# A hybrid decoder layer on eight cores: the norms as two sequences each, and attention's first query and key projections released by the first parked residual tile

## The chip, the cores and the metric

The kernel runs on the 8 cores of one Trainium2 chip. Each core computes one of the 8 batch elements with the same program and the same weights; the cores exchange nothing. The metric is the device time of the slowest core in microseconds (us), lower is better.

## The reference, cut to what is computed

```python
h = x + 0.5 * swiglu(rmsnorm(x, g1), w_gate_up1, w_down1)        # D=1024, D_FF=2816
u = rmsnorm(h, g_mix)
hg_q, hg_f, hg_i, hg_og, att_qkv, gate_A, gate_B = split(u @ w_in)
y_A = hgrn2(...)       # 4 heads, 128x128 state, chunks of 64, own norm and output gate
y_B = attention(...)   # 3 groups (window, dilation) = (128,1), (512,4), (2048,16), 8 heads of 64 each,
                       # causal, ALiBi; group outputs are joined by their softmax denominators
h = h + (sigmoid(gate_A) * (y_A @ w_A) + sigmoid(gate_B) * (y_B @ w_B)) @ w_out
h = h + 0.5 * swiglu(rmsnorm(h, g2), w_gate_up2, w_down2)
out = rmsnorm(h, g_final)
# rmsnorm(x, g) = x * rsqrt(mean(x*x) + 1e-6) * g;  x: (8, 2048, 1024) float32
```

## The kernel before, in words

**Layout.** A core keeps its 2048 tokens as 4 token tiles `tt` of 512, features on the partitions (8 chunks `c` of 128). The residual `hT` is one 64 KB-per-partition tile of float32 at offset H0, stored tile by tile; the normalized activations `xnT` are bf16 behind it. Weights are loaded in bf16 by POOL's DMA queue; the residual is parked in DRAM ("spill", L447) and the result stored (`store`, L453) by SP's queue.

**The planner.** Nothing is written out in engine order. Nineteen generators ("streams", list at L1141) yield small chunks of instructions or the name of an event to wait for. `schedule` (L182) takes, again and again, the chunk with the smallest key: its earliest start by a cost model (clock of its engine, readiness of its operands) plus the bias of its stream plus `P.extra`, a surcharge that a stream can put on its next chunk. Committed chunks go to the end of their engine's queue. Events order the commits only; what an instruction waits for on the chip comes from records (`Tok`, L31), one per buffer or part of one, that hold the last writer and the readers. `place` (L313) puts a buffer over older ones and takes over their records' readers and writers. Every engine's queue is in order. The planner takes 2 us plus bytes at 300 per ns for a DMA, 720 ns for a scalar-tensor-tensor (STT) of 512 columns on VectorE (DVE), 216 ns for a matmul of 512 columns.

**The norms.** `norm_stream` (L411) serves all four norms ("0" before the first feed-forward part, "1" before the mixer, "2" before the second feed-forward part, "3" the final one, in place). For each tile it squares the 8 chunks (`s_sq`, two buffers), adds each into bank 7 by a matmul with ones, takes Ln into `lnv` and Exp into bank 6, and multiplies the 8 chunks by gain and factor (8 STTs, surcharge 900 for norms 1 to 3 except on the last tile). Only then does it start the squares of the next tile. For norm 3 the last tile is done in two halves of 256 columns, as the last down projection is, yet both halves share one record per chunk.

**The first feed-forward part** (`ffn_stream`, L471) goes through gate-up and down weights in three groups. The last group's down projections (`down`, L509) go tile by tile: 8 pieces `m` of 8 matmuls, each followed by an STT into `hT`. Banks: 0 to 3 gate-up, 4, 5, 2, 3 the last downs, 7 norm sums, 6 norm factors.

**Around the change.** After that part the recurrence (`hg_proj` L569, `hg_vog` L636, `hg_state` L683) and attention run side by side. `hg_vog` projects values through bank 7 and waits for the event "norm1_done". `hg_state` needs them; its banks are 1 and 2. `at_load` (L801) waits for "ffn0_done" and "norm1_done", places attention's buffers over the residual (query and key tiles over residual tile 0, the others over tiles 1 to 3) and its weights over the down weights, sets the ones of the value tiles, and issues the bias and three weight DMAs (query, key, value) of each of 12 rounds `k`. `at_proj` (L837) projects them per round, 12 tiles of 8 matmuls through bank 3 (banks 2 and 3 once the recurrence is done), ScalarE (ACT) copies each out; `at_units` (L886) does scores and sums.

**The tail.** The second feed-forward part is the same code; its last down projections run over tiles 0, 1, 2 and the two halves of tile 3, and norm 3 and the stores follow.

Of the kernel before, what the change touches and what calls it, by code (L numbers as in the profile page):

```python
# [274 lines left out]
def build_program():  # L275
# [18 lines left out]
    with ExitStack() as st:  # L294
# [73 lines left out]
        hT_t = toks(8, 4)  # L368
        xn_t = toks(8, 4)
# [9 lines left out]
        hT = place("hT0", [128, 4, 8, 512], F32, H0, hT_t)  # L379
# [13 lines left out]
        def load_x():  # L393
            pre = ffn_pre(0)
            for tt in range(4):
                for q in range(4 if tt == 0 else 2):
                    n_ = 2 if tt == 0 else 4
                    DMA("pool", hT[:, tt, q * n_:(q + 1) * n_, :], xT_d[tt, :, q * n_ * 512:(q + 1) * n_ * 512], P.dsem(),
                        n_ * 262144, writes=[hT_t[c][tt] for c in range(q * n_, (q + 1) * n_)])
                    yield None  # L400
# [10 lines left out]
        def norm_stream(tag, gcol, inplace, after):  # L411
            for tt, lo, hi in ((0, 0, 512), (1, 0, 512), (2, 0, 512)) + (((3, 0, 256), (3, 256, 512)) if inplace else ((3, 0, 512),)):
                n_ = hi - lo
                for c in range(8):
# [5 lines left out]
                    if eng == "act":  # L420
                        ACT(sq[c % 2][:, 0:n_], h_[:, tt, c, lo:hi], AF.Square, [hT_t[c][tt]], [sq_t[c % 2]], n_)
                    else:
                        TT(eng, sq[c % 2][:, 0:n_], h_[:, tt, c, lo:hi], h_[:, tt, c, lo:hi], ALU.mult, [hT_t[c][tt]], [sq_t[c % 2]], costs[eng])
# [6 lines left out]
                yield None  # L430
                for c in range(8):
                    o_, ot = (h_[:, tt, c, lo:hi], hT_t[c][tt]) if inplace else (xnT[:, c, tsl(tt)], xn_t[c][tt])
                    STT(o_, h_[:, tt, c, lo:hi], vecs[:, gcol + c:gcol + c + 1], banks[6][:, 0:n_], ALU.mult, ALU.mult,
                        [hT_t[c][tt], bt[6], vecs_t], [ot], 55.0 + n_ * 1.3)
                    P.extra = 900.0 if tag != "0" and tt < 3 else 0.0
# [5 lines left out]
                P.events.add("xn%s_%d" % (tag, tt))  # L441
                if not inplace and after is not None:
                    after(tt)
                    yield None
            P.events.add("norm%s_done" % tag)

        def spill(tt):  # L447
            DMA("sp", hsp_d[tt], box["hT"][:, tt, :, :].rearrange("p c t -> p (c t)"), P.dsem(), 2097152,
                reads=[hT_t[c][tt] for c in range(8)], writes=[hsp_t[tt]])
# [3 lines left out]
        def store(tt, q, lo, hi):  # L453
            DMA("sp", outT_d[tt, :, q * 2048:(q + 1) * 2048].rearrange("p (c t) -> p c t", c=4)[:, :, lo:hi],
                box["hT"][:, tt, q * 4:(q + 1) * 4, lo:hi],
                out_ds[tt * 2 + q + (2 if lo else 0)], 2048 * (hi - lo), reads=[hT_t[c][tt] for c in range(q * 4, (q + 1) * 4)])
# [14 lines left out]
        def ffn_stream(which, xtag, htag):  # L471
# [37 lines left out]
            def down(grp, m, tt, dbs, lo=0, hi=512):  # L509
# [3 lines left out]
                for jj in range(n):  # L513
# [5 lines left out]
                    [bt[db], hT_t[m][tt]], [hT_t[m][tt]], 30.0 + (hi - lo) * 1.29)  # L519
# [281 lines left out]
        def at_load():  # L801
            yield "ffn0_done"
            yield "norm1_done"
# [6 lines left out]
            tmp_t, pT_t, acc_t = toks(2), toks(2, 4), toks(2, 4)  # L810
            at["qR"] = [place("qR%d" % i, [128, S], BF16, H0 + i * 4096, qR_t[i]) for i in range(2)]
            at["kR"] = [place("kR%d" % i, [128, S], BF16, H0 + 8192 + i * 4096, kR_t[i]) for i in range(2)]
            at["va"] = [place("vaug%d" % i, [128, 16, 2, 128], BF16, H0 + 16384 + i * 8192, va_t[i], vone_t[i]) for i in range(2)]
# [4 lines left out]
            at.update(qR_t=qR_t, kR_t=kR_t, vT_t=vT_t, va_t=va_t, vone_t=vone_t, tmp_t=tmp_t, pT_t=pT_t, acc_t=acc_t)  # L818
# [4 lines left out]
            for k in range(12):  # L823
# [6 lines left out]
                for s_ in range(3):  # L830
                    if k >= 1:
                        yield "part_%d_%d" % (k - 1, s_)
# [407 lines left out]
```

How the kernel before makes its waits and increments, by code:

```python
        def run(e, h):  # L234
            waited = {}
            for i, o in enumerate(prog.ops[e]):
                for ev in o["waits"]:
                    if ev[0] == "E":
                        sem, val, key = prog.esem[ev[1]], prog._resolve(ev), ("E", ev[1])
                    else:
                        sem, val, key = ev[1].h, ev[2], ("D", id(ev[1]))
                    if waited.get(key, 0) >= val:
                        continue
                    waited[key] = val
                    h.wait_ge(sem, val)
                if o["fn"] is None:
                    continue
                inst = o["fn"](h)
                if o["kind"] == "d":
                    inst.then_inc(o["ds"].h, 16)
                elif i in prog.needed[e]:
                    inst.then_inc(prog.esem[e], 1)
```

## Time and profile before

| | us |
|---|---|
| median of 3 runs | 1766.26 |
| all runs | 1763.83, 1766.26, 1945.64 |
| the profiled execution | 1766.38 |
| its span, slowest core (core 4), first to last instruction | 1764.8 |
| spans of the eight cores | 1757.6 to 1764.8 |
| TensorE busy (95% of the span) | 1674.9 |
| VectorE (DVE), ScalarE (ACT), GpSimd (POOL) busy | 769.3, 618.6, 167.4 |
| mean granted TensorE clock, core 4 | 0.980 |

The profile is one execution, seen on its slowest core. In its rows L336 is the helper through which all matmuls go, L342 ScalarE's activations, L348 the STTs, L360 the DMAs; the names `out<-in` tell them apart. "PEld" is TensorE's weight load, beside its matmuls. "x8" is a count; brackets or the part behind the bar give the idle time of the engine just before and what ended it. Matmuls are pipelined, so a matmul's own length (0.38 us) is more than its share of time.

### The profile page before, as it was taken

The page shows a single profiled execution, that of the slowest core. Times are in us where ns is not written, and L with a number is a line of the kernel's source. Part 1 is how long each engine was busy: PE and PEld are TensorE (multiplying, and loading weights), DVE is VectorE, ACT ScalarE, POOL GpSimd, SP SyncE. Part 2 cuts the span into 40 slices and gives each one's busy share as a digit, 9 for nine tenths or more (in the row PEclk, how much of TensorE's full clock was granted, in tenths as well). Part 3 has the DMA queues.
Part 4 walks back from the last instruction along what each step waited for, and adds up shares of the span by engine and source line. Part 5 has one row for each costly group of instructions (what it writes and reads, how often), then busy time and mean ns, then how long its engine had stood idle before and what let it go on. Part 6 is the DMA issues. An engine that isn't in the chain of part 4 may idle for free.

```text
span 1764.8 us, 25674 instructions; the slowest of 8 cores (1757.6 to 1764.8 us)
## 1 busy us (share of the span) xinstructions
PE 1674.9 (95%) x8556; PEld 765.3 (43%) x8556; DVE 769.3 (44%) x1248; ACT 618.6 (35%) x1044; POOL 167.4 (9%) x315
## 2 busy tenths in 40 slices
PE   6999999999989898899999999799999999999996
PEld 2444444444434444444444444344444444444443
DVE  4424223312465565764555445554632322331245
ACT  4310110011335666666575575522421011001123
POOL 2200101100003333310000000000010010010000
PEclk9999999999989899999999999799999999999997
DMA  8420427320240000022221222652042032132013
GB/s 230 78 36 13 66 37 120 60 36 13 96 126 13 7 12 14 1 55 45 34 37 22 52 40 38 161 122 36 1 66 48 13 59 44 24 57 40 12 48 144
DMA packets 29600, 95.17 MB, mean 54 GB/s; under 512 B 3232, under 2 KB 5408, under 8 KB 26912
## 3 DMA queue, kind: packets, MB, share of 16 engines
q0 software_dynamic: 23472, 65.19, 21.6%
q1 hardware_dynamic: 6000, 28.34, 4.5%
q8 instruction: 73, 1.20, 0.3%
q14 instruction: 55, 0.45, 0.1%
HBM read 133.52 MB, written 16.78 MB: 85 GB/s over the span
## 4 chain that ended last, share of the span: by engine, by line
PE 88%; ACT 6%; issue 3%; DVE 2%; POOL 0%; DMA 0%; DVEq 0%; ACTq 0%; POOLq 0%
PE bank L336 87%; ACT s_fin L342 1%; ACT s_sq L342 1%; PE bank L339 1%; ACT s_T L342 1%; ACT s_lnv L342 1%; DVE s_hT L348 1%; DVE s_tmp L345 1%; ACT s_vT L342 0%; ACT L342 0%; DMA s_hT<-xT 0%; DVE s_T L620 0%; ACT s_vaug L342 0%; ACT s_kR L342 0%; DVE s_S L348 0%
## 5 line engine op out<-in xcount | busy, mean ns | idle before, releaser
L336 PE MATMUL bank<-s_xnT,s_wgu 128*128 128x512 bf16 x2816 | 618.7, 381 | 2.7 <-DVE s_xnT L348 2.4
L336 PEld LDWEIGHTS bank<-s_xnT,s_wgu 128*128 128x128 bf16 x2816 | 276.6, 98 | 340.2 <-issue 12.2
L342 ACT ACTIVATE s_sg<-bank 128x512 f32<-128x512 f32 x176 | 105.0, 597 | 659.0 <-PE bank L336 657.3
L345 DVE TENSOR_TENSOR s_actT<-s_sg,bank 128x512 bf16<-128x512 f32 x176 | 120.9, 688 | 463.4 <-PE bank L336 463.4
L336 PE MATMUL bank<-s_actT,s_wd 128*128 128x512 bf16 (+1 forms) x1472 | 309.3, 370 | 0.0
L336 PE MATMUL bank<-s_xnT,s_watt 128*128 128x512 bf16 x1152 | 285.3, 384 | 12.9 <-ACT s_kR L342 5.8
L348 DVE SCALAR_TENSOR_TENSOR s_hT<-bank,s_hT 128x512 f32<-128x512 f32 (+1 forms) x232 | 156.2, 673 | 195.0 <-PE bank L336 194.7
L336 PEld LDWEIGHTS bank<-s_actT,s_wd 128*128 128x128 bf16 x1472 | 143.7, 98 | 157.9 <-issue 0.6
L336 PEld LDWEIGHTS bank<-s_xnT,s_watt 128*128 128x128 bf16 x1152 | 105.0, 98 | 135.2 <-issue 30.9
L336 PE MATMUL bank<-s_xnT,s_wm 128*128 128x512 bf16 x512 | 128.0, 385 | 6.0 <-ACT s_sA L342 6.0
L345 DVE TENSOR_TENSOR s_tmp<-bank,s_bias 128x512 f32<-128x512 f32 (+1 forms) x200 | 104.4, 553 | 53.4 <-PE bank L336 40.1
L342 ACT ACTIVATE s_sq<-s_hT 128x512 bf16<-128x512 f32 (+1 forms) x121 | 69.0, 595 | 142.7 <-PE bank L336 88.9
L342 ACT ACTIVATE s_pT<-s_tmp 128x512 bf16<-128x512 f32 (+1 forms) x160 | 93.7, 601 | 53.2 <-DVE s_tmp L345 51.0
L336 PE MATMUL bank<-s_xnT,s_whg 128*128 128x512 bf16 x384 | 93.1, 379 | 0.5 <-ACT s_v L342 0.5
L336 PE MATMUL bank<-s_sq,s_ones_bf 128*128 128x512 bf16 (+1 forms) x136 | 51.3, 408 | 31.0 <-ACT s_sq L342 18.1
L336 PEld LDWEIGHTS bank<-s_xnT,s_wm 128*128 128x128 bf16 x512 | 48.9, 99 | 63.5 <-issue 12.3
L348 DVE SCALAR_TENSOR_TENSOR s_xnT<-s_hT,s_vecs,bank 128x512 bf16<-128x512 f32 x96 | 66.4, 741 | 13.6 <-ACT bank L342 13.6
L360 POOL DMA_DIRECT2D s_wgu<-wgu x44 | 23.3, 531 | 495.6 <-PE bank L336 495.4
L342 ACT ACTIVATE s_sA<-bank 128x512 f32<-128x512 f32 x64 | 38.1, 595 | 75.8 <-PE bank L336 73.7
L345 DVE TENSOR_TENSOR s_acc<-s_acc,bank 128x512 f32<-128x512 f32 x64 | 54.8, 892 | 22.3 <-PE bank L336 22.0
L351 POOL TENSOR_SCALAR s_Sb<-s_S,s_dcs 128x128 bf16<-128x128 f32 x112 | 48.1, 431 | 159.5 <-DVE s_S L348 107.0
L336 PE MATMUL bank<-s_mT,s_wo 128*128 128x512 bf16 x256 | 59.8, 379 | 0.0
(87 smaller groups left out, 1164.5 us busy)
## 6 DMA issues: line engine op xcount, KB each, us to landing
s_wgu<-wgu POOLq DMA_DIRECT2D x44, 512.0 KB, 5.2
s_wd<-wd POOLq DMA_DIRECT2D x44, 256.0 KB, 9.6
s_watt<-watt POOLq DMA_DIRECT2D x36, 256.0 KB, 4.0
hsp<-s_hT SPq DMA_DIRECT2D x4, 2048.0 KB, 6.3
s_hT<-hsp SPq DMA_DIRECT2D x4, 2048.0 KB, 25.5
s_hT<-xT POOLq DMA_DIRECT2D x6, 1024.0 KB, 26.4
outT<-s_hT SPq DMA_DIRECT2D x6, 1024.0 KB, 4.3
s_whg<-whg POOLq DMA_DIRECT2D x8, 512.0 KB, 21.0
```

What stands on the lines that cost most here:

```text
L336: P.op("pe", lambda h: h.matmul(out, lhsT=lhsT, rhs=rhs, start=start, stop=stop, skip_group_check=skip), reads, writes, mm_ns(n))
L339: P.op("pe", lambda h: h.transpose(out, in_, ident_), reads, writes, mm_ns(128))
L342: P.op("act", lambda h: h.activation(out=out, in_=in_, func=func, **kw), reads, writes, act_ns(n), TABLES.get(func))
L345: P.op(eng, lambda h: h.tensor_tensor(out=out, in0=in0, in1=in1, op=op), reads, writes, ns)
L348: P.op("dve", lambda h: h.scalar_tensor_tensor(out=out, in0=in0, scalar=scalar, in1=in1, op0=op0, op1=op1), reads, writes, ns)
L351: P.op(eng, lambda h: h.tensor_scalar(out=out, in0=in0, scalar1=s1, scalar2=s2, op0=op0, op1=op1), reads, writes, ns)
L360: return lambda h: h.dma_start(out=out, in_=in_)
```

## The change

1. `norm_stream` becomes two streams for each norm. `norm_sum` does squares, sums, Ln and Exp; `norm_apply` does the STTs and what follows them. The Exp writes banks in turn (6 and 5; 6 and 1; 6 alone; 6 and 0), and from the point where a bank is used again the sum sequence waits for the event that its earlier factors are applied. The sum streams of norms 1 and 3 get bias -700 (the other streams of the norms -300). The surcharge of 900 now also stands on the first half of norm 3's last tile.
2. The last 256 columns of the residual's tile 3 get records of their own (`hTb_t`), and every access goes through `ht(c, tt, lo, hi)`; the placements of the residual list their records per tile.
3. `at_load` waits for "norm1_done" later. The three weight DMAs of round 0 come at "ffn0_done"; the query and key tiles are placed once tile 0 is parked (event "sp_0"); the other buffers, the ones and the bias wait for "norm1_done" as before. `at_proj` starts at "at_qk", waits before each tile for that tile's normalized activations, and for "at_ready" before the first value projection.

```diff
+        hTb_t = toks(8)
+        def ht(c, tt, lo=0, hi=512):
+            if tt < 3:
+                return [hT_t[c][tt]]
+            return ([hT_t[c][tt]] if lo == 0 else []) + ([hTb_t[c]] if hi == 512 else [])
...
-        hT = place("hT0", [128, 4, 8, 512], F32, H0, hT_t)
+        hT = place("hT0", [128, 4, 8, 512], F32, H0, hT_t, hTb_t)
+        placed[-1:] = [(H0 + tt * 16384, H0 + (tt + 1) * 16384, [t for c in range(8) for t in ht(c, tt)]) for tt in range(4)]
...
-        def norm_stream(tag, gcol, inplace, after):
-            for tt, lo, hi in ((0, 0, 512), (1, 0, 512), (2, 0, 512)) + (((3, 0, 256), (3, 256, 512)) if inplace else ((3, 0, 512),)):
+        def norm_sum(tag, inplace, rbanks):
+            for i, (tt, lo, hi) in enumerate(norm_parts(inplace)):
                 n_ = hi - lo
+                rb = rbanks[i % len(rbanks)]
                 for c in range(8):
...
                     MM(banks[7][:, 0:n_], ones_bf[:], sq[c % 2][:, 0:n_], c == 0, c == 7, [sq_t[c % 2], ones_t], [bt[7]], n_)
                     yield None
+                if i >= len(rbanks):
+                    yield "na%s_%d" % (tag, i - len(rbanks))
                 ACT(lnv[:, 0:n_], banks[7][:, 0:n_], AF.Ln, [bt[7]], [lnv_t], n_, scale=1.0 / D, bias=EPS)
                 yield None
-                ACT(banks[6][:, 0:n_], lnv[:, 0:n_], AF.Exp, [lnv_t], [bt[6]], n_, scale=-0.5)
-                yield None
+                ACT(banks[rb][:, 0:n_], lnv[:, 0:n_], AF.Exp, [lnv_t], [bt[rb]], n_, scale=-0.5)
+                yield None
+                P.events.add("ns%s_%d" % (tag, i))
+
+        def norm_apply(tag, gcol, inplace, rbanks, after):
+            for i, (tt, lo, hi) in enumerate(norm_parts(inplace)):
...
+                yield "ns%s_%d" % (tag, i)
+                h_ = box["hT"]
                 for c in range(8):
...
-                    P.extra = 900.0 if tag != "0" and tt < 3 else 0.0
+                    P.extra = 900.0 if tag != "0" and hi < 512 or tt < 3 and tag != "0" else 0.0
...
+                P.events.add("na%s_%d" % (tag, i))
                 if not inplace and after is not None:
                     after(tt)
                     yield None
+                    P.events.add("sp_%d" % tt)
...
         def at_load():
             yield "ffn0_done"
-            yield "norm1_done"
...
+            for s_ in range(3):
+                first(0, s_)
+                yield None
+                P.events.add("watt_0_%d" % s_)
+            yield "sp_0"
             at["qR"] = [place("qR%d" % i, [128, S], BF16, H0 + i * 4096, qR_t[i]) for i in range(2)]
             at["kR"] = [place("kR%d" % i, [128, S], BF16, H0 + 8192 + i * 4096, kR_t[i]) for i in range(2)]
+            at.update(qR_t=qR_t, kR_t=kR_t)
+            P.events.add("at_qk")
+            yield "norm1_done"
...
         def at_proj():
-            yield "at_ready"
+            yield "at_qk"
...
                 for s_ in range(3):
                     yield "watt_%d_%d" % (k, s_)
...
+                    if s_ == 2 and k == 0:
+                        yield "at_ready"
...
                     for tt in range(4):
+                        yield "xn1_%d" % tt
                         B = nextb()
...
-            Stream("n0", norm_stream("0", 0, False, None), -300.0),
+            Stream("n0", norm_sum("0", False, (6, 5)), -300.0),
+            Stream("a0", norm_apply("0", 0, False, (6, 5), None), -300.0),
...
-            Stream("n1", norm_stream("1", 8, False, spill), -300.0),
+            Stream("n1", norm_sum("1", False, (6, 1)), -700.0),
+            Stream("a1", norm_apply("1", 8, False, (6, 1), spill), -300.0),
...
-            Stream("n3", norm_stream("3", 24, True, store), -300.0),
+            Stream("n3", norm_sum("3", True, (6, 0)), -700.0),
+            Stream("a3", norm_apply("3", 24, True, (6, 0), store), -300.0),
```

## Rows read from the trace of the kernel before

**Rows 1.** The page's chain that ended last, shares of the span by engine

```profile
PE 88%; ACT 6%; issue 3%; DVE 2%; POOL 0%; DMA 0%; DVEq 0%; ACTq 0%; POOLq 0%
```

**Rows 2.** Busy time by stretch; the first line names the columns

```profile
core 4: us, PE busy (x) PEld busy (x) DVE busy (x) ACT busy (x) POOL busy (x), PEclk, DMA share, GB/s
440.00:506.00 66.00, 65.53 (x302) 29.13 (x301) 37.33 (x55) 23.61 (x39) 2.55 (x2) 1.00 0.23 96
506.00:524.00 18.00, 11.54 (x31) 2.98 (x28) 11.40 (x17) 9.25 (x16) 1.65 (x3) 0.72 0.76 190
540.00:800.00 260.00, 234.85 (x1501) 111.99 (x1499) 165.55 (x329) 167.35 (x293) 74.00 (x143) 0.97 0.11 18
1225.00:1300.00 75.00, 74.07 (x338) 32.43 (x337) 38.57 (x57) 29.39 (x45) 2.35 (x5) 1.00 0.04 9
...
1740.00:1765.00 25.00, 8.14 (x23) 2.24 (x22) 16.12 (x31) 12.34 (x28) 0.00 (x0) 0.62 0.67 252
```

**Rows 3.** Start of the kernel, the same columns, 50 to 54 us

```profile
50.00:54.00 4.00, 2.02 (x6) 0.67 (x7) 3.47 (x6) 2.35 (x4) 3.12 (x5) 0.88 0.00 0
```

**Rows 4.** Instructions in order of time, end of the first feed-forward and after

```profile
506.59 0.69 DVE L348 SCALAR_TENSOR_TENSOR s_hT<-bank,s_hT 128x512 f32<-128x512 f32 x1 [1.47 <-PE bank L336]
...
507.10 1.65 POOL L360 DMA_DIRECT2D s_watt<-watt  x3 [17.92 <-PE bank L336]
507.37 0.32 SPq L360 DMA_DIRECT2D hsp<-s_hT  x1
...
510.02 5.36 DVE L348 SCALAR_TENSOR_TENSOR s_xnT<-s_hT,s_vecs,bank 128x512 bf16<-128x512 f32 x8 [2.74 <-ACT bank L342]
...
516.91 3.57 PE L336 MATMUL bank<-s_whg,s_xnT 128*128 128x512 bf16 x8 [0.84 <-ACT s_lnv L342]
```

**Rows 5.** Chain of waits, one round of down projection, sum and square

```profile
446.51 0.23 issue
446.74 0.70 DVE s_hT L348
...
447.64 0.64 ACT s_sq L342
...
448.41 0.59 PE bank L336 x2
```

**Rows 6.** Page, DMA issues: operation, count, KB each, median us to landing

```profile
s_watt<-watt POOLq DMA_DIRECT2D x36, 256.0 KB, 4.0
hsp<-s_hT SPq DMA_DIRECT2D x4, 2048.0 KB, 6.3
```

**Rows 7.** The attention weights' tile: issue to landing, window 500 to 530

```profile
DMA to landing us min/median/max: 11.3/13.2/14.8
```

**Rows 8.** DMA answer, window 507 to 525, issues and time to landing

```profile
hsp<-s_hT SPq DMA_DIRECT2D x1, 2048.0 KB, 11.2
```

**Rows 9.** Two single microseconds of the same stretch, columns as in Rows 2

```profile
511.00:512.00 1.00, 0.70 (x2) 0.10 (x1) 1.00 (x2) 0.72 (x2) 0.00 (x0) 0.50 1.19 236
521.00:522.00 1.00, 0.68 (x4) 0.35 (x5) 1.00 (x3) 0.18 (x1) 0.00 (x0) 1.00 0.95 240
```

**Rows 10.** Instructions in order of time, the tail

```profile
1739.96 0.42 DVE L348 SCALAR_TENSOR_TENSOR s_hT<-bank,s_hT 128x256 f32<-128x256 f32 x1 [0.45 <-PE bank L336]
...
1740.30 4.03 DVE L348 SCALAR_TENSOR_TENSOR s_hT<-s_hT,s_vecs,bank 128x512 f32<-128x512 f32 x6
...
1746.09 5.35 DVE L348 SCALAR_TENSOR_TENSOR s_hT<-s_hT,s_vecs,bank 128x512 f32<-128x512 f32 x8 [1.77 <-ACT bank L342]
...
1755.69 0.81 ACT L342 ACTIVATE s_sq<-s_hT 128x256 bf16<-128x256 f32 x2 [0.22 <-PE bank L336]
...
1758.15 3.22 DVE L348 SCALAR_TENSOR_TENSOR s_hT<-s_hT,s_vecs,bank 128x256 f32<-128x256 f32 x8 [2.90 <-ACT bank L342]
```

**Rows 11.** Groups by shape, window 1726 to 1766

```profile
L348 DVE SCALAR_TENSOR_TENSOR s_hT<-bank,s_hT 128x256 f32<-128x256 f32 x16 | 6.8, 424 | 7.0 <-PE bank L336 7.0
...
L342 ACT ACTIVATE s_sq<-s_hT 128x256 bf16<-128x256 f32 x16 | 6.1, 411 | 2.2 <-PE bank L336 1.6 <-DVE s_hT L348 0.7
```

More of the change, by code:

```diff
@@ L398, in load_x @@
                     DMA("pool", hT[:, tt, q * n_:(q + 1) * n_, :], xT_d[tt, :, q * n_ * 512:(q + 1) * n_ * 512], P.dsem(),
-                        n_ * 262144, writes=[hT_t[c][tt] for c in range(q * n_, (q + 1) * n_)])
+                        n_ * 262144, writes=[ht(c, tt) for c in range(q * n_, (q + 1) * n_)])
                     yield None
@@ L409, in load_x, with norm_parts @@
                     P.events.add("h0_%d_%d_0" % (c, tt))
-        def norm_stream(tag, gcol, inplace, after):
-            for tt, lo, hi in ((0, 0, 512), (1, 0, 512), (2, 0, 512)) + (((3, 0, 256), (3, 256, 512)) if inplace else ((3, 0, 512),)):
+        def norm_parts(inplace):
+            last = ((3, 0, 256), (3, 256, 512)) if inplace else ((3, 0, 512),)
+            return ((0, 0, 512), (1, 0, 512), (2, 0, 512)) + last
+        def norm_sum(tag, inplace, rbanks):
+            for i, (tt, lo, hi) in enumerate(norm_parts(inplace)):
                 n_ = hi - lo
+                rb = rbanks[i % len(rbanks)]
                 for c in range(8):
@@ L448, in spill @@
             DMA("sp", hsp_d[tt], box["hT"][:, tt, :, :].rearrange("p c t -> p (c t)"), P.dsem(), 2097152,
-                reads=[hT_t[c][tt] for c in range(8)], writes=[hsp_t[tt]])
+                reads=[ht(c, tt) for c in range(8)], writes=[hsp_t[tt]])
         out_ds = [P.dsem() for _ in range(10)]
@@ L455, in store @@
                 box["hT"][:, tt, q * 4:(q + 1) * 4, lo:hi],
-                out_ds[tt * 2 + q + (2 if lo else 0)], 2048 * (hi - lo), reads=[hT_t[c][tt] for c in range(q * 4, (q + 1) * 4)])
+                out_ds[tt * 2 + q + (2 if lo else 0)], 2048 * (hi - lo), reads=[ht(c, tt, lo, hi) for c in range(q * 4, (q + 1) * 4)])
         ffn_box = {}
@@ L810, in at_load, with first @@
             tmp_t, pT_t, acc_t = toks(2), toks(2, 4), toks(2, 4)
+            def first(k, s_):
+                DMA("pool", at["w"][s_][:], watt_d[k // 3, 2 - k % 3, s_], dsw[s_], 524288, writes=[w_t[s_]])
+            for s_ in range(3):
[3 more added lines that the diff above has]
+            yield "sp_0"
             at["qR"] = [place("qR%d" % i, [128, S], BF16, H0 + i * 4096, qR_t[i]) for i in range(2)]
             at["kR"] = [place("kR%d" % i, [128, S], BF16, H0 + 8192 + i * 4096, kR_t[i]) for i in range(2)]
+            at.update(qR_t=qR_t, kR_t=kR_t)
+            P.events.add("at_qk")
+            yield "norm1_done"
             at["va"] = [place("vaug%d" % i, [128, 16, 2, 128], BF16, H0 + 16384 + i * 8192, va_t[i], vone_t[i]) for i in range(2)]
@@ L1106, in wout_load @@
                 DMA("sp", box["hT"][:, tt, :, :].rearrange("p c t -> p (c t)"), hsp_d[tt], P.dsem(), 2097152, reads=[hsp_t[tt]],
-                    writes=[hT_t[c][tt] for c in range(8)])
+                    writes=[ht(c, tt) for c in range(8)])
                 yield None
@@ L1128, in wout @@
                     h_ = box["hT"]
-                    STT(h_[:, tt, m, :], banks[db][:], 0.5, h_[:, tt, m, :], ALU.mult, ALU.add, [bt[db], hT_t[m][tt]], [hT_t[m][tt]], 690.0)
+                    STT(h_[:, tt, m, :], banks[db][:], 0.5, h_[:, tt, m, :], ALU.mult, ALU.add, [bt[db], ht(m, tt)], ht(m, tt), 690.0)
                     yield None
```

36 lines of the change are left out of this document (20 added, 16 removed).

## The prediction

> **What bounds the kernel now.** I read the page's summary of the chain that ended last first: 88% of the span is TensorE work [rows 1]. Then the busy time by stretch, to find where TensorE is *not* full, since only there can a reordering give time back. There are four such places that the change can reach [rows 2, 3]: the start; the end of the first feed-forward part (506 to 524 us); the recurrence stage (540 to 800 us, 234.85 busy of 260, so 25 us idle); and the tail (8.14 busy of 25). The last tiles of the first feed-forward part before 506 us are full (65.53 of 66), and so is the stretch with the third norm (74.07 of 75).
>
> The profiled execution took 1766.38 us, 1.6 us more than its span of 1764.8, and lies 0.1 us from the median of the three runs, 1766.26. I sum against 1766.4.
>
> **Step 1, first norm as two sequences (start).** Squares of a tile no longer wait until the eight normalizing STTs of the tile before are committed, and the factors alternate between banks 6 and 5. From 50 to 54 us TensorE is busy 2.02 of 4 us: it waits for squares of the last tile, which came behind the STTs of the third [rows 3]. At best these 2 us go. Against it: squares committed earlier carry their sum matmuls earlier into TensorE's queue, and if the planner's landing time for x is too early the queue stands behind them. No row prices that; the nearest is the longest time a full set of eight STTs holds DVE, 5.36 us [rows 4], and I take half of it, 3, as the upper end. Value: -1 (range -2 to +3), nearer the idle that a row shows.
>
> **Step 2, second norm and its last tile.** With the squares at -700 and their own stream, seven of the last tile's eight sums and the rest of the third tile's move in front of the last down projection. Before, twelve sums came behind it. A matmul of 512 columns takes 0.217 us (65.53 us over 302 of them [rows 2]), so the last down projection ends 11 x 0.217 = 2.4 us later: at about 508.7 instead of 506.3, which is where its STT starts, 506.59 [rows 4], less a hand-over of 0.2. From there the last STT, square and sum take 1.9 us [rows 5], the factors about 1.3, the eight STTs 5.36. So the last normalized tile is there at 517.5 instead of 523.3. That is a real 5.8 us, if somebody uses it.
>
> **Step 3, who uses it.** The change wants the first query and key projections there. They need three things: the residual's first tile parked (the first of four spills, of 6.3 us each in the median [rows 6], issued long before), normalized tiles 0 to 2 (there), and their weights. The weights' issue now stands behind the gate "norm1_done" in the order of commits, yet on the chip it does *not* wait for it: the three issues start at 507.10, right behind the last down projection, whose weights lay in that memory; the row names TensorE as releaser [rows 4]. So the edit moves these DMAs in the planner's account only; POOL has nothing else in front of them. And they land late: 11.3, 13.2 and 14.8 us after issue [rows 7], against a median of 4.0 over all 36 [rows 6], because the spill of the fourth residual tile, 2 MB, is issued 0.3 us behind, at 507.37 [rows 4], and itself takes 11.2 us instead of 6.3 [rows 8]. Both are tied to the same last down projection and stay side by side after the change.
>
> So query weights come at 508.7 + 0.8 + 11.3 = 520.8 us. The planner, with 2 us plus bytes at 300 per ns, expects them 4.0 us after the last down projection, and so commits query tiles 0 and 1 ahead of the recurrence's first value projection, which gets its turn only when the last STT of the norm is committed, at 8.3 us by the planner's costs. TensorE's queue is in order. Before, that value projection started at 516.91, released by the logarithm that read bank 7 [rows 4]; it could now start near 511. Instead it stands behind two query tiles that wait for weights.
>
> The sum. Before, from 506 to 524 us, 31 matmuls [rows 2] of 0.217 us, 6.7 us of work, stand in 18 us: 11.3 us lost. After: from 508.9 to 520.8 nothing, 11.9 us; then the clock. It was 0.50 (1.2 GHz) in the idle stretch of before and came back to 1.00 (2.4 GHz) by 521, 4 us after the value projections began [rows 9]; the longer idle will do the same, which costs half of 3.7 us, 1.8; and 0.84 us between two tiles through the single bank 3. Together 14.5, or +3. The value projection starts at 520.8 + 3.5 + 0.8 + 1.7 = 526.8, ten us late, with 2.5 tiles more of attention done than before at the same point of the recurrence. I take +3. Bounds: -6 if the weights come in 4.0 us (lost: 4.6 us to 513.5 and 1 for bank 3, 5.6 against 11.3), and +13 if the recurrence's delay of 9.5 us is paid in full and the weights take 14.8 us.
>
> The Trainium skill has a rule here: "DMA: Bandwidth & Descriptors", section on the anatomy of a DMA of the gpsimd path, gives 2.0 us plus the bytes at 436 GB/s, an estimate of 2.6 to 3.2 us for 256 KB written from 512 KB read. By it the fill would work and the sum be that of the first rival. The trace of before has 11.3 us for the first of them, and the measurement decides. The same page (queues, rings and completion order) says that the engines take turns between queues packet by packet, which fits the doubled time of the spill.
>
> **Step 4, fourth norm and tail.** Here the old single sequence hurt most. With 256-column pieces the down STTs win every turn from the postponed STTs (+900), so six of the second tile's and all of the third tile's STTs stay until the last piece, at 1739 us, and the squares stand behind them. DVE then works 4.03, 5.35, 3.22 and 3.22 us one after another, with gaps for the norm chain [rows 10]; the second half's squares even waited for the other half's STTs, as both shared one record.
>
> After: squares and sums run along. Eight sums of 512 and fifteen of 256 columns come in front of the end of the last down piece: 8 x 0.217 + 15 x 0.11 = 3.4 us. They also set a pace: a square-and-sum round takes 1.90 us from the end of the down matmuls to the sum [rows 5]; with the halves' STT 0.27 shorter and square 0.23 shorter [rows 11] that is 1.4 us, and the order puts 0.87 (a down piece, 13.8 us of DVE busy and idle over 16 [rows 11]) + 0.11 = 0.98 us of matmuls between, so TensorE waits up to 0.4 on each second piece, 3.2 us over sixteen; the postponed STTs of 0.74 us now fit about one per piece, since a piece lasts longer, and make DVE 0.42 + 0.74 = 1.16 us a piece. I take 3.5 us of waits. The last down piece ended at 1739.7, a hand-over before its STT at 1739.96 [rows 10]; now at 1739.7 + 3.4 + 3.5 = 1746.6. Behind it: STT and hand-over 0.8, then what before took from the last pair's second square (1756.1) to the end of the span, 8.7 us [rows 10]. End 1756.1, -8.7; what is left of the earlier tiles' STTs hides in the 3 us of the norm chain. I take -8.5. Bounds: -12 without any wait; -0.5 with waits of 5 us and every STT of the last two tiles still behind the last piece (5.4 + 3.2 + 3.2 + 3.4 us after 1749).
>
> **The rest.** The third norm keeps one bank, in a full stretch: 0, covered by TensorE's work there [rows 2]. The four spills, the memsets of the value tiles and the biases keep their places in their queues. Recurrence and attention are planned anew from 510 us on; that stage has 25 us of idle in small pieces, and the new order can move a few of them either way: 0, +-3. What is late next in the middle: the transposes and state chain, ten us later than before, with attention ahead.
>
> **Sum.** -1 + 3 - 8.5 = -6.5: 1759.9, say 1760.
>
> **The rivals.** (a) *The fill works.* The weights land in about 4 us, because the spill waits longer or the queues share otherwise. Middle -6 instead of +3: 1751. For it: the median of 4.0; against it: the same two transfers collided in before, from the same releaser. (b) *The value projection behind the weights costs more than the tail gives.* The place is TensorE's queue at 509 us. Each us that the recurrence starts later is paid at the end if attention, done ahead, lacks as filler later; then +9.5, and with the last weights' time of 14.8 us +13: 1766.4 - 1 + 13 - 8.5 = 1770, slower. It decides from a middle of +9.5 on. For it: 25 us of idle in the recurrence, where latency rules; against it: from 800 us on TensorE is again nearly full, so work done ahead is work saved. (c) *The tail keeps its starving.* The STTs behind the last piece stay, the waits come on top: tail -2, 1766.4 - 1 + 3 - 2 = 1766. For it: the postponement of 900 is still there; against it: with sums between the pieces the down STT comes later than the postponed key.
>
> **How the numbers follow.** Forecast 0.5, (a) 0.17, (b) 0.18, (c) 0.15. The range goes from (a) less some of the replanning, 1748, to (b), 1771. A measurement of this kernel tells about 2%, 35 us, from no change; no case comes near that: faster 0.02, same 0.96, slower 0.02.
>
> **What would show it.** Right: the three weight issues near 509.5 us with landings of 11 us and more; TensorE idle from 509 to 520 us at clock 0.50, first query matmul near 521, first value projection near 527; the last down piece near 1746 and a single group of eight half STTs behind it. Wrong: query matmuls at 513 us; value projections ahead of the queries; idle in 540 to 800 us up by over 5 us; more than one group of 512-column STTs behind the last down piece.

## The result, and the profile after

The changed kernel took 1776.2 us in the median of its runs (1774.27 to 1777.02), the kernel before 1763.8 in the same comparison: a ratio of 1.0067, with a 95% interval of 1.0054 to 1.008. Some executions are slowed, with one die at a lower granted clock (1945.64 us of the kernel before is one), and all medians here leave them out. The changed kernel is 12 us slower, less than what this kernel's measurement calls a change, yet clear of its spread. I had forecast 1760 with a range up to 1771. The profiled execution took 1777.02 us with a span of 1775.4: 10.6 us more than the 1764.8 of before.

First the page of the changed kernel: the chain that ended last, by engine and by line, and the group of the attention projections.

```profile
PE 85%; ACT 6%; issue 3%; DVE 3%; DMA 2%; POOL 1%; ACTq 0%; DVEq 0%; POOLq 0%
PE bank L336 84%; DMA s_watt<-watt 1%; ACT s_fin L342 1%; ACT s_T L342 1%; ACT s_lnv L342 1%; ACT s_sq L342 1%; PE bank L339 1%; ACT L342 1%; ACT s_vT L342 0%; DVE s_tmp L345 0%; DVE s_hT L348 0%; POOL s_Sb L351 0%; DMA s_wgu<-wgu 0%; DMA s_hT<-xT 0%; DVE s_T L645 0%
...
L336 PE MATMUL bank<-s_xnT,s_watt 128*128 128x512 bf16 x1152 | 284.5, 383 | 24.4 <-DMA s_watt<-watt 13.7
```

TensorE's share of the chain fell from 88% [rows 1] to 85%, and a transfer is in the chain that was not there: the attention weights. The group says the same from the other side: of 24.4 us in which TensorE stood ahead of these projections, 13.7 ended with that DMA. Then the stretches, in the columns of [rows 2, 3]:

```profile
50.00:54.00 4.00, 2.40 (x8) 0.82 (x8) 2.91 (x5) 1.93 (x3) 3.10 (x5) 0.82 0.08 2
440.00:506.00 66.00, 63.93 (x293) 27.77 (x290) 38.77 (x56) 30.07 (x48) 2.54 (x2) 1.00 0.23 96
506.00:524.00 18.00, 5.64 (x24) 2.22 (x24) 12.92 (x16) 3.09 (x5) 1.66 (x3) 0.70 0.70 175
...
540.00:800.00 260.00, 230.83 (x1492) 109.61 (x1490) 164.78 (x335) 162.69 (x283) 76.35 (x150) 0.98 0.10 16
1225.00:1300.00 75.00, 74.64 (x339) 32.62 (x338) 39.05 (x59) 29.04 (x43) 1.58 (x3) 1.00 0.13 22
1300.00:1330.00 30.00, 27.70 (x112) 11.00 (x111) 11.81 (x18) 9.30 (x13) 3.79 (x8) 0.94 0.40 57
1740.00:1776.00 36.00, 22.45 (x164) 15.22 (x162) 22.23 (x46) 11.02 (x25) 0.00 (x0) 0.91 0.42 158
```

Three things are to be seen against those of before. The gap behind the first feed-forward part is emptier (5.64 busy of 18, before 11.54). The tail is fuller, as meant. And there is a hole in a stretch that I had not looked at, 1300 to 1330 us: 2.3 us idle with the clock at 0.94, where before has:

```profile
1300.00:1330.00 30.00, 30.00 (x141) 13.62 (x139) 11.37 (x17) 7.79 (x12) 2.92 (x6) 1.00 0.69 114
```

The timeline of the changed kernel at the end of the first feed-forward part answers to [rows 4]:

```profile
510.13 0.69 DVE L348 SCALAR_TENSOR_TENSOR s_hT<-bank,s_hT 128x512 f32<-128x512 f32 x1 [0.59 <-PE bank L336]
...
510.62 1.66 POOL L360 DMA_DIRECT2D s_watt<-watt  x3 [22.26 <-PE bank L336]
...
510.90 0.32 SPq L360 DMA_DIRECT2D hsp<-s_hT  x1
...
511.80 0.38 PE L336 MATMUL bank<-s_sq,s_ones_bf 128*128 128x512 bf16 x1 [1.27 <-ACT s_sq L342]
...
513.66 5.35 DVE L348 SCALAR_TENSOR_TENSOR s_xnT<-s_hT,s_vecs,bank 128x512 bf16<-128x512 f32 x8 [2.19 <-ACT bank L342]
...
523.12 3.57 PE L336 MATMUL bank<-s_xnT,s_watt 128*128 128x512 bf16 x8 [10.95 <-DMA s_watt<-watt]
...
527.59 1.89 PE L336 MATMUL bank<-s_xnT,s_watt 128*128 128x512 bf16 x8 [0.89 <-ACT s_qR L342]
...
529.31 1.89 PE L336 MATMUL bank<-s_whg,s_xnT 128*128 128x512 bf16 x8
```

TensorE's last sum is at 511.80, its next work at 523.12: 10.95 us of waiting for the query weights. The first query tile takes 3.57 us, the second 1.89 for the same eight matmuls: that is the clock, 0.50 in the microsecond before and back after it. The recurrence's first value projection stands behind both, at 529.31, 12.4 us later than the 516.91 of before. The spill of the last residual tile (the hsp row) is issued 0.3 us behind the loads, as before [rows 4], and the three loads took, by the view of their tile from 500 to 530 us,

```profile
DMA to landing us min/median/max: 12.3/12.6/15.2
```

against 11.3/13.2/14.8 [rows 7]; the spill took 12.2 us (11.2 before [rows 8]).

**Where the 10.6 us are.** I cut the span at landmarks that both kernels have: the first transposes of the recurrence, the first and last output projection of the mixer, the last gate-up matmul. In a row of a tile's instructions, the two numbers behind the durations are the first and the last start. Before:

```profile
L339 PE MATMUL bank<-s_cstb,s_kg x64: 216/219/314, 529.4 to 746.3; 128*128 128x128 bf16 x64
...
L336 PE MATMUL bank<-s_mT,s_wo x256: 376/379/379, 1215.1 to 1296.4; 128*128 128x512 bf16 x128
...
L336 PE MATMUL bank<-s_xnT,s_wgu x1408: 378/379/379, 1254.1 to 1680.2; 128*128 128x512 bf16 x176
```

After:

```profile
L339 PE MATMUL bank<-s_cstb,s_kg x64: 216/219/219, 540.2 to 757.0; 128*128 128x128 bf16 x64
...
L336 PE MATMUL bank<-s_mT,s_wo x256: 376/379/379, 1224.1 to 1314.8; 128*128 128x512 bf16 x128
...
L336 PE MATMUL bank<-s_xnT,s_wgu x1408: 376/379/634, 1257.4 to 1695.9; 128*128 128x512 bf16 x176
```

The transposes come 10.8 us late. From them to the first output projection it is 683.9 us instead of 685.7, so 1.8 us came back and 9.0 stay. From there to the last gate-up matmul it is 471.8 instead of 465.1, 6.7 us more: a second loss, where I had put 0. From there to the end it is 79.5 instead of 84.6, a gain of 5.1. Together 9.0 + 6.7 - 5.1 = 10.6.

These are the slowest core of either profile, and the cores differ. Where the last group's down projections begin, near 436 us, the eight cores of either kernel lie over 4 us apart (434.6 to 438.7 us before, 434.4 to 439.2 after; middle of the eight 435.5 and 435.7), and the slowest core of before is one of the late ones. By the middle of the eight cores the transposes come 13.3 us late and the first output projection 9.9; the other two distances hardly differ between cores (470.4 to 472.4 and 79.1 to 79.5 us after, 465.0 to 465.1 and 84.5 to 85.0 before).

### The profile page after: what moved, and what is told of

Same layout as the page of the kernel before. It is cut to its first block, busy times and chain, and to the rows that moved or that the text cites. A ratio compares the mean times of both kernels' runs of the same rounds, so it can differ in the third digit from the quotient of the medians.

```text
span 1775.4 us, 25698 instructions; the slowest of 8 cores (1763.9 to 1775.4 us)
## 1 busy us (share of the span) xinstructions
PE 1676.0 (94%) x8556; PEld 764.0 (43%) x8556; DVE 768.5 (43%) x1249; ACT 621.9 (35%) x1042; POOL 168.4 (9%) x316
## 4 chain that ended last, share of the span: by engine, by line
PE 85%; ACT 6%; issue 3%; DVE 3%; DMA 2%; POOL 1%; ACTq 0%; DVEq 0%; POOLq 0%
PE bank L336 84%; DMA s_watt<-watt 1%; ACT s_fin L342 1%; ACT s_T L342 1%; ACT s_lnv L342 1%; ACT s_sq L342 1%; PE bank L339 1%; ACT L342 1%; ACT s_vT L342 0%; DVE s_tmp L345 0%; DVE s_hT L348 0%; POOL s_Sb L351 0%; DMA s_wgu<-wgu 0%; DMA s_hT<-xT 0%; DVE s_T L645 0%
## 5 line engine op out<-in xcount | busy, mean ns | idle before, releaser
L336 PE MATMUL bank<-s_actT,s_wd 128*128 128x512 bf16 (+1 forms) x1472 | 315.0, 370 | 0.0
L336 PE MATMUL bank<-s_xnT,s_watt 128*128 128x512 bf16 x1152 | 284.5, 383 | 24.4 <-DMA s_watt<-watt 13.7
L336 PEld LDWEIGHTS bank<-s_xnT,s_wm 128*128 128x128 bf16 x512 | 48.9, 99 | 63.8 <-issue 12.2
```

Source lines behind the costliest of these rows:

```text
L336: P.op("pe", lambda h: h.matmul(out, lhsT=lhsT, rhs=rhs, start=start, stop=stop, skip_group_check=skip), reads, writes, mm_ns(n))
```

## The experiments

The kernels below were timed against the kernel before on the same chip, in four comparisons: e1 to e4, e5 to e8, e9 to e11, and e12. Between comparisons the column of differences counts. In e5 to e8 the recorded ratios lie up to 0.002 under those of the two medians, and two runs of the kernel before took 1782 us there.

| run | what differs from the changed kernel | us | minus the kernel before | ratio to before (95%) |
|---|---|---|---|---|
| changed kernel | | 1776.2 | +12.4 | 1.0067 (1.0054 to 1.008) |
| e1 | attention's early start undone | 1763.4 | -1.1 | 0.999 (0.998 to 1.0001) |
| e2 | all four norms single again | 1780.4 | +15.9 | 1.0089 (1.0074 to 1.0104) |
| e3 | third norm single | 1771.2 | +6.7 | 1.0041 (1.0024 to 1.0058) |
| e4 | query weights loaded early | 1764.3 | -0.2 | 0.9995 (0.9985 to 1.0005) |
| e5 | last spill behind the weights | 1769.5 | +4.8 | 1.0006 (0.998 to 1.0032) |
| e6 | e4 and e3 | 1759.4 | -5.4 | 0.9965 (0.9933 to 0.9998) |
| e7 | e1 and e3 | 1755.6 | -9.2 | 0.9928 (0.9894 to 0.9961) |
| e8 | before, with the fourth norm split and the records of part 2 | 1759.1 | -5.7 | 0.9948 (0.9923 to 0.9974) |
| e9 | e6, one query tile ahead only | 1755.7 | -8.5 | 0.995 (0.9935 to 0.9964) |
| e10 | e6 and e5 | 1757.1 | -7.1 | 0.997 (0.995 to 0.999) |
| e11 | e7, attention held back | 1767.7 | +3.5 | 1.0028 (1.0008 to 1.0048) |
| e12 | e9, third norm split, gate-up held | 1755.5 | -8.3 | 0.9949 (0.9936 to 0.9962) |

**e1, early start undone.** All norms stay split.

```diff
         def at_load():
             yield "ffn0_done"
+            yield "norm1_done"
...
-            yield "at_qk"
+            yield "at_ready"
```

> The changed kernel with its part 3 undone (attention waits for norm1_done again; all four norms stay two sequences). Theory A: the middle loses because the recurrence's first value projection stands in TensorE's queue behind query projections whose weights are not there, and the recurrence sets the pace until attention's end. Then here the value projections start near 513 us, the recurrence's first transposes near 525 (before 529.4, changed kernel 540.2), and the sum is 1765 - 0.8 (start) - 4 (middle) + 6.7 (third norm) - 5.1 (tail) = 1762. Theory B: the split of the second norm itself (sums and waits between the last down projections) and the new plan behind it cost the middle: about 1774, as the changed kernel.

Measured 1763.4, 12.8 below the changed kernel. The first value projection is at 513.9 and the first transposes at 526.1, 14.1 us before those of the changed kernel; 12.8 of them are left at the first output projection (1211.3). The early start costs that. The splits alone are 1 us ahead of the kernel before, which the interval doesn't tell from nothing: the third norm's loss (470.9 us from the first output projection to the last gate-up, 465.1 before) stands against the tail's gain.

**e2, the early start with single norms.** The split's streams are replaced by the one of before.

```diff
-            Stream("n1", norm_sum("1", False, (6, 1)), -700.0),
-            Stream("a1", norm_apply("1", 8, False, (6, 1), spill), -300.0),
+            Stream("n1", norm_stream("1", 8, False, spill), -300.0),
```

and so for the other three.

> Part 3 alone: all norms as single sequences, attention released as in the changed kernel. Theory A: the queue has five half tiles of the query projection before the value projections, so these start near 527 and the middle loses 10 to 13 us, all else as before: 1765 + 11 = 1776. Theory B: without the splits little changes: 1763 to 1768.

Measured 1780.4, worse than the changed kernel and than the 1776 expected. Here TensorE's queue has the weights' wait in front of the last tile's own sums, in its timeline:

```profile
518.80 3.57 PE L336 MATMUL bank<-s_xnT,s_watt 128*128 128x512 bf16 x8 [10.37 <-DMA s_watt<-watt]
...
528.53 0.59 PE L336 MATMUL bank<-s_sq,s_ones_bf 128*128 128x512 bf16 x2
...
534.35 3.14 PE L336 MATMUL bank<-s_whg,s_xnT 128*128 128x512 bf16 x7 [0.84 <-ACT s_lnv L342]
```

The sums of the norm that the value projection needs come at 528.5, behind the projections, and the value projection at 534.4. So the parts belong together: the early start costs 16 us without the splits (e2 against before), and 13 with them (the changed kernel against e1).

**e3, third norm single.** The same replacement for norm 2 alone.

> The changed kernel with the third norm (before the second feed-forward part) as one sequence again. Theory A: its split spends the first gate-up projections of the second feed-forward part in between the output projections, so that nothing covers the last tile's norm; that costs 6.7 us of the changed kernel: 1776 - 6.7 = 1769.5. Theory B: the 6.7 us there are a late effect of the middle (other landing times of weights): 1775 to 1777.

Measured 1771.2, 5.0 less. From the first output projection to the last gate-up matmul it is now 465.1 us, as in before, so the stage gives back all of its 6.7.

**e4, query weights early.** The first round's query weights get a place of their own and are loaded some 240 us earlier; the bias whose place they take goes where they had been.

```diff
         def at_load():
-            yield "ffn0_done"
+            yield "dn0_1"
...
+            at["w"] = [place("watt0", [128, 1024], BF16, X0 + 106496, w_t[0])]
+            DMA("pool", at["w"][0][:], watt_d[0, 2, 0], dsw[0], 524288, writes=[w_t[0]])
+            yield None
+            P.events.add("watt_0_0")
+            yield "ffn0_done"
```

> The changed kernel with the first query weights in the memory of bias buffer 0, which is free, and the bias where the query weights were: the query weights are loaded during the first feed-forward part. Theory A: the fill then works; three query tiles run from 510.5 us on, the value projections start near 518 instead of 529, the recurrence's first transposes near 528 instead of 540, and 11 to 12 us come back: 1776 - 11 = 1765. Theory B: less than 3 us come back: 1773 to 1776.

Measured 1764.3, 12 less, from the weights' wait alone. Its timeline of TensorE:

```profile
509.99 0.38 PE L336 MATMUL bank<-s_sq,s_ones_bf 128*128 128x512 bf16 x1 [1.29 <-ACT s_sq L342]
510.23 1.89 PE L336 MATMUL bank<-s_xnT,s_watt 128*128 128x512 bf16 x8
513.00 1.89 PE L336 MATMUL bank<-s_xnT,s_watt 128*128 128x512 bf16 x8 [0.89 <-ACT s_qR L342]
515.73 1.89 PE L336 MATMUL bank<-s_xnT,s_watt 128*128 128x512 bf16 x8 [0.84 <-ACT s_qR L342]
517.45 1.89 PE L336 MATMUL bank<-s_whg,s_xnT 128*128 128x512 bf16 x8
```

The query tiles fill the gap as the change meant, at 1.89 us each, and the value projection starts at 517.45, 12 us before that of the changed kernel.

**e5, last spill behind the weights.** Only the fourth spill's issue waits for the three loads.

```diff
-                reads=[ht(c, tt) for c in range(8)], writes=[hsp_t[tt]])
+                reads=[ht(c, tt) for c in range(8)] + (at["w_t"] if tt == 3 and "w_t" in at else []), writes=[hsp_t[tt]])
```

> The changed kernel with the spill of the fourth residual tile waiting until the three weight loads of round 0 have landed. Theory A: the weights were late because they shared the DMA engines with this spill (11.3 to 14.8 us against 4.0 in the median of all); alone they land 4 to 5 us after issue, the query projections start near 515 instead of 523, value projections near 521, the recurrence 7 to 8 us earlier, and 7 us come back: 1769. Rival: they are slow by themselves (three at once, behind each other on POOL's queue, with the biases): landing stays over 9 us and the time within 2 us of 1776.

Measured 1769.5, 6.7 less. The loads, in the window of their tile, took

```profile
DMA to landing us min/median/max: 5.2/5.9/7.1
```

instead of 12.3/12.6/15.2, and the first query tile starts at 514.01 instead of 523.12 (the issue is itself 2.1 us earlier on the core shown). So what SP issued beside the loads made them late. That is the spill, but not it alone: two bias loads of 256 KB stand behind it in SP's queue, issued at 511.27 in the changed kernel and at 517.18 here, and the run doesn't separate them from the spill.

**e6, e7 and e8: which parts are worth having.** e6 joins e4 and e3; e7 keeps all splits but the third norm's and undoes the early start; e8 is the kernel before with the fourth norm split and the separate records for the last 256 columns that this needs.

> Query weights early (as in the fourth experiment) and the third norm as one sequence: both repairs in the changed kernel. If they are independent, 1764.4 - 6.5 = 1758, that is 7 us faster than before. If the third norm's cost was tied to the state the middle leaves behind, 1762 or more.

> Part 3 undone and the third norm as one sequence; first, second and fourth norm stay split: 1763.7 - 6.5 = 1757, 8 us faster than before. If the costs are not additive, 1760 to 1764.

> Only the fourth norm as two sequences, with the records of the last halves; all else as before. The tail from the last gate-up matmul to the end of the span takes 79.5 us instead of 84.6: 1765.3 - 5.1 = 1760. If the tail's gain belonged to another part (the planner's state), 1764 to 1766.

Measured 1759.4, 1755.6 and 1759.1: each as expected within 2 us. By e8 the fourth norm alone carries 6 us. e7, which has the first two norms split as well, is 3.5 us faster in the same comparison; which of the two gives that was not run. e6 is 3.8 us slower than e7, with intervals that touch: even with the weights early, the early start adds nothing that these times show. The tail also tells part 2 from part 1: from the last gate-up matmul to the end it is 84.6 us before, 83.4 in e2, which has the separate records for the last 256 columns but no split, and 79.7 in e8.

**e9, one tile ahead; e10, the spill moved as well.**

```diff
                     for tt in range(4):
                         yield "xn1_%d" % tt
+                        if k == 0 and s_ == 0 and tt == 1:
+                            yield "hv_0"
```

so that only one query tile goes ahead of the first value projection; e10 is e6 with e5's line.

> As the sixth experiment (query weights early, third norm single), but only the first query tile goes ahead of the value projections; the others wait until the values of tile 0 are done. If the recurrence's start decides, its transposes come at 525.5 as in the seventh (530.3 in the sixth), and the time is that of the seventh, 1757, or 1 less for the tile done in idle time. If attention's head start is what counts, it loses against the sixth: 1761 or more.

> The sixth with the fourth tile's spill behind the key and value weights. These then land within 7 us, but nothing waits for them in the sixth before 524 us: within 1.5 us of the sixth, 1758 to 1761, if only the order of the queue matters; 1755 or less if late key weights cost there too.

Measured 1755.7 for e9 and 1757.1 for e10 of the same comparison, with intervals that overlap. In e9 the value projection is at 513.1, in e6 at 519.5; each query tile ahead of it holds the recurrence up by some 2.7 us (e4's timeline). That this costs time in the end is probable and not shown. e10 can't be told from e6 either: with the query weights there early, no effect of the spill is left to see.

**e11, attention held back.** My theory by now: the mixer is as long as the recurrence, and attention only fills. Then attention may also start late. e7, with its projections behind the recurrence's first head block:

```diff
             yield "at_ready"
+            yield "hb_0"
```

> The seventh (splits but for the third norm, part 3 undone) with attention's first projections held back until the recurrence's first unit is done: three to four projection tiles, 5 to 7 us of TensorE work, that ran before it run later. Theory A (the recurrence paces the stage, attention's tiles are filler that finds idle time later too): first transposes a little earlier, total 1757 to 1759. Rival (work done ahead is work saved, as the prediction had it): 1762 to 1764.

Measured 1767.7, beyond what either side had expected: 12 to 13 over e7. The first query matmul came at 542.2 instead of 524.7, and from the first transposes to the first output projection it is 693.4 us instead of 684.9 (690.0 instead of 684.6 in the middle of the eight cores). The theory fell in this form: attention is no slack. Starting it 17.5 us later cost 8.5 us in that stage.

**e12, third norm split with its filler kept.** The loss of 6.7 us in that norm could be the split itself or TensorE's order behind it. The timeline of TensorE and DVE in the kernel before:

```profile
1296.65 1.89 PE L336 MATMUL bank<-s_xnT,s_wgu 128*128 128x512 bf16 x8
...
1298.80 29.52 PE L336 MATMUL bank<-s_xnT,s_wgu 128*128 128x512 bf16 x136
...
1301.95 5.36 DVE L348 SCALAR_TENSOR_TENSOR s_xnT<-s_hT,s_vecs,bank 128x512 bf16<-128x512 f32 x8 [0.46 <-ACT bank L342]
```

and in the changed one:

```profile
1315.03 1.89 PE L336 MATMUL bank<-s_xnT,s_wgu 128*128 128x512 bf16 x8
...
1317.13 3.61 PE L336 MATMUL bank<-s_xnT,s_wgu 128*128 128x512 bf16 x16
1320.96 0.38 PE L336 MATMUL bank<-s_xnT,s_wgu 128*128 128x512 bf16 x1 [0.22 <-DVE s_xnT L348]
1321.62 0.38 PE L336 MATMUL bank<-s_xnT,s_wgu 128*128 128x512 bf16 x1 [0.28 <-DVE s_xnT L348]
...
1320.07 5.36 DVE L348 SCALAR_TENSOR_TENSOR s_xnT<-s_hT,s_vecs,bank 128x512 bf16<-128x512 f32 x8 [2.35 <-ACT bank L342]
```

The eight STTs of the last tile are the same 5.36 us. Before, they lie under an unbroken run of 136 gate-up matmuls. Of the gate-up matmuls, 144 need only the three finished tiles. Before, 80 of them stand ahead of the last group of output projections and 64 behind it: the 8 at 1296.65 and the first 56 of the 136. After, 120 stand ahead, which is also why the last output projection starts at 1314.8 instead of 1296.4, and 24 behind: the 8 at 1315.03 and the 16 at 1317.13. Then TensorE steps behind DVE, one matmul an STT. The 40 spent early are 40 x 0.217 = 8.7 us of work. From the first to the last output projection it is 9.4 us more than before, from there to the last gate-up only 2.7 us less: 6.7 lost. (The expectation of e12 counts 88 and 56 for before, as seen from the last sum, and 120 and 24 for after, as seen from the output projection. Its "32 projections, 7 us" mixes the two, and that it comes near 6.7 is chance.) e12 keeps the split and gives the filler back: the third tile's gate-up waits until the output projections are committed.

```diff
                 if which == 1:
                     yield "xn%s_%d" % (xtag, tt)
+                    if tt == 2:
+                        yield "w_done"
```

> As the ninth experiment, but with the third norm as two sequences again, and the second feed-forward part's first gate-up projections of token tile 2 held until the output projection is done. Then 88 of them stand between the output projections, as in the kernel before, and 56 behind (changed kernel: 120 and 24). If the split itself costs (more waits for squares), the stage from the first output projection to the last gate-up stays at 471 to 472 us and the time is 1762. If it costs because 32 projections, 7 us of work, were spent before the last tile's norm instead of behind it, the stage takes 465 to 466 us and the time is that of the ninth, 1756.

Measured 1755.5, no different from e9 with the single norm, and 465.9 us from the first output projection to the last gate-up matmul, with 80 and 64 gate-up matmuls before and behind as in the kernel before. It was the order.

## Why the prediction was wrong

Two terms failed: the credit for attention's work done ahead in step 3 (+3, and it was +9 to +10), and the third norm (0, and it was +6.7). The tail was mis-sized by 3.4. The +9.5 of rival (b) in place of the +3 would have given 1766.4, inside the range; the third norm and the tail's missing gain carry the result beyond it.

**Step 1 came out by luck.** On the slowest cores the last group's down projections start at 437.90 instead of 438.68: 0.8 us, forecast 1. But the cores spread over more than 4 us there, and the middle of the eight is at 435.7, before at 435.5, so no gain at the start is shown. The window from 50 to 54 is still only 2.40 us busy.

**Step 2 was right in its mechanism.** The last down projection's STT came 3.5 us later, not 2.4: the 11 sums, less the 0.8 by which that core was earlier, and 1.9 us in three stalls that the sums now cause between the pieces of the projection, in stretches that were full. I had costed the moved sums by their 0.217 us and not by the square that each waits for.

**Step 3 was right in its events and wrong in its sum.** Weights issued behind the last down projection: forecast 509.5, was 510.62. Landing of the first: forecast 11.3, was 12.3. Value projection: forecast 526.8, was 529.3. The clock fell to 0.50 in the wait, as said. The step that failed is the credit: "ten us late, with 2.5 tiles more of attention done", from which I took +3. What was there is +9.8 (9.0 late at the first output projection, and the 0.8 of the start lost too), or 9.9 by the middle of the eight cores. That is rival (b), forecast at +9.5, to which I gave 0.18.

Why the work done ahead paid so little is seen in the windows of the instructions on the attention weights (columns as above without DVE and ACT). Before:

```profile
540.00:600.00 60.00, 18.25 (x70) 6.17 (x67) 1.78 (x3) 0.97 0.10 14
600.00:680.00 80.00, 24.23 (x92) 8.59 (x92) 1.13 (x2) 0.96 0.07 12
680.00:700.00 20.00, 1.03 (x4) 0.39 (x4) 0.60 (x1) 1.00 0.10 14
740.00:760.00 20.00, 11.26 (x44) 3.89 (x42) 1.07 (x2) 0.91 0.17 27
```

After:

```profile
540.00:600.00 60.00, 15.97 (x66) 5.76 (x64) 1.73 (x3) 1.00 0.10 14
600.00:680.00 80.00, 23.67 (x96) 8.47 (x96) 1.73 (x3) 1.00 0.05 11
680.00:700.00 20.00, 0.00 (x0) 0.00 (x0) 0.00 (x0) 0.83 0.10 14
740.00:760.00 20.00, 8.07 (x32) 2.63 (x32) 0.00 (x0) 1.00 0.01 2
```

With those before 540 us both kernels have run 98 of these matmuls by 600 us. Two rounds of three projections are 192; the changed kernel has run them by 680 us, the one before lacks 4, and in the code the third round waits for the first round's attention units. It starts at 703.3 us before and at 706.0 after, and by 800 us the kernel before has run 381 of these matmuls, the changed one 344. "More attention done" held only beside the same point of the *recurrence*; in absolute time attention is no further, and by 800 us it is behind. I compared against the wrong clock: my +3 was the idle of TensorE up to the first projections, and not the delay of the recurrence. The 24 matmuls ahead at the transposes are 5.2 us of work; 1.8 us came back on the slowest core, and 3.4 by the middle of the eight.

What exactly sets the time from the transposes to the output projection is not settled. On the slowest core of each profile it is 683.1 to 685.8 us in before, in the changed kernel and in e1, e2, e3, e5, e6, e7, e8, e9 and e12, 680.4 in e4 and 693.4 in e11. The middles of the eight cores tell more: 684.6 with no query tile ahead (e7; 684.8 before), 682.8 with one (e9), 680.1 and 678.8 with three (e6, e4), 690.0 with attention held back (e11). So by these profiles each tile ahead gives back some 1.5 to 2 us in that stage, while one in front of the value projection delays the recurrence by 2.7. That attention and recurrence are both near the limit there is a reading that these runs allow but don't prove.

**The bound of the weights' time** was in the trace of before [rows 7, 8], and e5 fits the cause named there: with the spill, and the two bias loads behind it, held back the loads take 5.2 to 7.1 us. The Trainium skill ("DMA: Bandwidth & Descriptors", anatomy of a DMA of the gpsimd path) gives 2.0 us plus the bytes at 436 GB/s, an estimate of 2.6 to 3.2 us for these loads; the median of all these loads is 4.0 [rows 6], and beside the spill the rule is off by a factor of about four. The shortest of the 36 loads took 3.5 us in either kernel, so none here meets it.

**Step 4, the tail, was mis-sized.** Forecast -8.5, measured -5.1 (4.9 to 5.5 in the runs with this norm split). The end was nearly exact: from the last down piece to the end of the span 9.3 us, where I had summed 9.5 (0.8 + 8.7), and one group of eight STTs of 0.4 us stands there instead of the four groups of [rows 10]. The timeline of the changed kernel:

```profile
1766.19 0.42 DVE L348 SCALAR_TENSOR_TENSOR s_hT<-bank,s_hT 128x256 f32<-128x256 f32 x1 [0.34 <-PE bank L336]
...
1766.54 0.86 DVE L348 SCALAR_TENSOR_TENSOR s_hT<-s_hT,s_vecs,bank 128x256 f32<-128x256 f32 x2
...
1767.75 0.38 ACT L342 ACTIVATE s_lnv<-bank 128x256 f32<-128x256 f32 x1 [0.51 <-PE bank L336]
...
1768.71 3.22 DVE L348 SCALAR_TENSOR_TENSOR s_hT<-s_hT,s_vecs,bank 128x256 f32<-128x256 f32 x8 [1.31 <-ACT bank L342]
```

But the last down piece itself is pushed back further than the 3.4 + 3.5 = 6.9 us forecast. From the last gate-up matmul to the end of that piece it is 69.8 us with 65.10 busy, before 59.2 with 59.19:

```profile
1696.30:1766.10 69.80, 65.10 (x359) 33.92 (x356) 41.63 (x70) 26.46 (x48) 0.00 (x0) 1.00 0.24 98
```

So the last down piece ends 10.6 us later. The sums that now stand in front of it are 8 of 512 and 14 of 256 columns, 3.3 us at 0.217 and 0.11 us each; the other 7.3 are waits, where I had 3.5. The profile shows 4.7 of them as idle. The rest hides in the busy time: a sum of 256 columns is shown with 0.27 us, though what follows it without a wait starts 0.11 later (the sum at 1752.51, the next matmul at 1752.62), so a matmul's row reaches into the wait behind it. That the squares would set the pace was forecast; the waits came to twice what I had put.

**The third norm failed outright.** "The third norm keeps one bank, in a full stretch: 0, covered by TensorE's work there." The stretch that I read for it (1225 to 1300, 74.07 of 75 busy) is as full after; the cover was spent inside it, and the loss came behind it, where I had not looked: +6.7. A busy engine in the stretch of a change doesn't cover it, if what keeps it busy is the filler of the next stretch.

With the measured terms: -0.8 + 9.8 + 6.7 - 5.1 = 10.6; the first two are one number, +9.0, as no gain at the start is shown.

## What to carry to other kernels

In a queue that works in order, work placed ahead on a planner's belief in a transfer time makes everything behind it as late as the transfer really is: look up the landing time where the move puts it, beside the transfers issued with it, and load such an operand early (e4: 12 us). Credit for work done ahead has to be worked out in absolute time and up to the next gate that holds that work. And filler is a stock: if a norm's work may start earlier, see what it leaves for the wait behind it; holding one tile's filler back (e12) kept the split harmless. A gain or loss under a few us on one core is to be looked up on all eight first: the 0.8 of step 1 was the luck of a core. The best versions here, e7, e9 and e12, are 8.3 to 9.2 us faster than the kernel before and can't be told apart; of the change, e7 keeps the splits of three norms and the separate records.

## What I had not expected of the hardware

That the three loads of 256 KB take 5.2/5.9/7.1 us instead of 12.3/12.6/15.2 once the 2 MB store is held back was expected; that the store itself, issued behind them, still took 8.8 us and not the 6.3 of the median [rows 6], was not. Two bias loads are issued 0.4 us behind it; whether they are the cause is open. The clock: in the changed kernel's gap it was 0.50 and the first query tile took 3.57 us; in e4 the same gap, filled with tiles of 1.89 us and pauses of 0.84 to 0.89 between them, kept it at 1.00:

```profile
511.00:512.00 1.00, 1.00 (x6) 0.29 (x3) 0.14 (x1) 0.66 (x2) 0.00 (x0) 1.00 0.95 324
```
